# A two-layer hybrid backbone on one core: gathers between the turn of the activations and the down products, and the turn of a modulation group as a step of its own

## The reference

```python
for l in range(DEPTH):                       # DEPTH = 2, context and latent tokens alike
    sh1, sc1, g1, sh2, sc2, g2 = adaln_params(c, w_mod[l], b_mod[l])  # silu(c) @ w_mod: 1024 x 6144
    h = rmsnorm(x, ln1_g[l]) * (1 + sc1) + sh1
    conv, attention, mLSTM inputs and gates = split(h @ w_in[l])
    x = x + g1 * (concat(conv_o, na_o, ml_o) @ w_out[l])
    h2 = rmsnorm(x, ln2_g[l]) * (1 + sc2) + sh2
    # 16 experts in 4 groups: best group, 2 experts in it
    a = silu(h2 @ w_gate[e]) * (h2 @ w_up[e])
    x = x + g2 * sum_e gate[e] * (a @ w_down[e])
```

## Time and profile before

| | |
|---|---|
| median of three runs | 1233.97 us (1231.61 to 1316.1) |
| the profiled execution | 1231.81 us, of which the span is 1230.0 us |
| PE busy | 1145.1 us, 93% of the span |
| DVE, ACT, POOL busy | 409.4, 250.2, 56.5 us |
| mean granted clock of PE | 0.975 |
| moved | 315.15 MB, mean 256 GB/s; read from HBM 310.92 MB |

### The profile page before, as it was taken

The page is one execution under the profiler, slowest core; times in us unless marked ns, Lnnn a source line. Parts: engine busy times, 40 slices in busy tenths (PEclk is TensorE's granted clock), DMA queues, the critical chain, the costliest instruction groups (busy, mean ns, idle before and its releaser), DMA issues.

```text
span 1230.0 us, 15289 instructions
## 1 busy us (share of the span) xinstructions
PE 1145.1 (93%) x6240; PEld 623.2 (51%) x6240; DVE 409.4 (33%) x1150; ACT 250.2 (20%) x515; POOL 56.5 (5%) x82
## 2 busy tenths in 40 slices
PE   3999999898989999999989999998998999999996
PEld 3546555576544533554434564566654554355333
DVE  4402041355270333223252302224727032322234
ACT  2210121152132010110142011214413201011013
POOL 1230000000002000000020000000000000000001
PEclk8999999999999999999999999999998999999998
DMA  8967452277248989999971346234425698999991
GB/s 318 357 131 285 167 206 99 95 269 234 80 201 304 409 319 412 413 413 413 404 264 69 137 161 229 99 137 172 117 72 205 251 410 319 411 412 413 413 379 52
DMA packets 95512, 315.15 MB, mean 256 GB/s; under 512 B 5980, under 2 KB 6352, under 8 KB 86608
## 3 DMA queue, kind: packets, MB, share of 16 engines
q1 hardware_dynamic: 91856, 306.43, 65.1%
q0 software_dynamic: 3584, 7.71, 2.7%
HBM read 310.92 MB, written 4.99 MB: 257 GB/s over the span
## 4 chain that ended last, share of the span: by engine, by line
PE 85%; DVE 8%; ACT 3%; issue 2%; POOL 1%; DMA 1%; SPq 0%; DVEq 0%; POOLq 0%; ACTq 0%
PE ps L1341 18%; PE ps L944 16%; PE ps L1388 9%; PE ps L954 9%; PE ps L1112 6%; PE ps L1179 5%; PE ps L901 3%; PE ps L1207 2%; PE ps L891 2%; PE ps L1208 2%; PE ps L1231 1%; PE ps L1078 1%; PE ps L1143 1%; PE ps L934 1%; PE ps L1005 1%
## 5 line engine op out<-in xcount | busy, mean ns | idle before, releaser
L944 PE MATMUL ps<-ring,hT 128*128 128x512 f32 (+1 forms) x480 | 194.9, 565 | 0.0
L1341 PE MATMUL ps<-ring,arena 128*64 128x512 f32 x576 | 175.4, 595 | 0.0
L2014 DVE SCALAR_TENSOR_TENSOR xT<-ps,modT,xT 128x128 f32<-128x128 f32 x320 | 109.3, 410 | 193.9 <-PE ps L1208 106.0
L1341 PE MATMUL ps<-slot,arena 128*64 128x512 f32 x368 | 147.4, 596 | 0.0
L944 PEld LDWEIGHTS ps<-ring,hT 128*128 128x128 f32 x480 | 90.5, 190 | 98.0 <-issue 94.7
L954 PE MATMUL ps<-hT,ring 128*128 128x384 f32 x320 | 106.2, 489 | 0.0
L1388 PE MATMUL ps<-ring,arena 128*64 128x512 f32 x336 | 88.5, 613 | 8.1 <-ACT arena L1673 8.1
L1341 PEld LDWEIGHTS ps<-ring,arena 128*64 128x64 f32 x576 | 52.2, 137 | 78.9 <-issue 78.9
L1112 PE MATMUL ps<-mixT,ring 128*128 128x384 f32 x256 | 83.4, 487 | 1.7 <-ACT mixT L1601 1.7
L2238 DVE SCALAR_TENSOR_TENSOR y_low<-ps,route,y_high 128x512 fp32r<-128x512 f32 x32 | 23.9, 751 | 173.3 <-ACT y_high L1679 172.6
L954 PEld LDWEIGHTS ps<-hT,ring 128*128 128x128 f32 x320 | 59.8, 190 | 40.7 <-issue 0.8
(11 more groups left out here) (332 smaller groups left out, 1294.5 us busy)
## 6 DMA issues: line engine op xcount, KB each, us to landing
ring<-in_w_mod SPq DMA_DIRECT2D x24, 2048.0 KB, 11.7
ring<-in_w_down SPq DMA_DIRECT2D x44, 1024.0 KB, 13.7
ring<-in_w_up SPq DMA_DIRECT2D x40, 1024.0 KB, 11.3
ring<-in_w_gate SPq DMA_DIRECT2D x32, 1024.0 KB, 12.8
slot<-in_w_gate SPq DMA_DIRECT2D x30, 1024.0 KB, 13.1
ring<-in_w_in SPq DMA_DIRECT2D x14, 2048.0 KB, 12.3
slot<-in_w_up SPq DMA_DIRECT2D x22, 1024.0 KB, 10.3
slot<-in_w_down SPq DMA_DIRECT2D x22, 1024.0 KB, 11.3
```

What stands on the lines that cost most here:

```text
L944: mm = pe.matmul(p[:, 0:n], hT[:, k, t * P:(t + 1) * P], w[:, k, c0:c0 + n], start=(k == 0), stop=(k == KT - 1))
L1341: mm = pe.matmul(out[which][64 * s:64 * s + 64, :], xg[:, k, cols[s]], w[i][:, k % 4, :], start=(k == 0), stop=(k == KT - 1))
L2014: ins = dve.scalar_tensor_tensor(xT[:, m, cols], p[:, cols], modT[:, L, gate0 + m, j:j + 1], xT[:, m, cols], ALU.mult, ALU.add)
```

## The change

Two things are moved; nothing is added or removed in the arithmetic.

In the pairs, `aT` comes before the gathers on PE and on ACT. In the mixing half, the turn of a group is a step `mod_turn` of its own, one step behind the group's last block: behind the context scores for group 1, behind the turn of the last probabilities for group 2, behind `read(6)` for the next layer's group 0. And the four blocks of the next layer's group stand ahead of the reads 0, 2, 4 and 6 instead of 1, 3, 5 and 7.

```diff
     for dh in range(8):
         steps += [("decay", dh + 1)] if dh < 7 else []
-        steps += mods[:1] if dh % 2 else []
+        steps += mods[:1] if dh % 2 == 0 else []
         steps += [("read", dh)]
-        if dh % 2:
+        if dh % 2 == 0:
             del mods[:1]
     assert not mods
+    for i in reversed([i for i, step in enumerate(steps) if step[0] == "mod" and step[2] % 4 == 3]):
+        steps.insert(i + 2, ("mod_turn", *steps[i][1:]))
     return steps
...
                     if c % 4 == 3:
                         done(mm, name)
-                        bk.wait_drained(pe, name)
-                        turned = ("modT", which, c // 4)
-                        p = begin(turned)
-                        for i in range(4):
-                            mm = pe.transpose(p[:, i * P:(i + 1) * P], modrow[:, i * P:(i + 1) * P], ident)
-                        done(mm, turned)
                     else:
                         mm.then_inc(ly.mod_read, 1)
+
+                def mod_turn(which, c):
+
+                    bk.wait_drained(pe, ("mod", which, c // 4))
+                    turned = ("modT", which, c // 4)
+                    p = begin(turned)
+                    for i in range(4):
+                        mm = pe.transpose(p[:, i * P:(i + 1) * P], modrow[:, i * P:(i + 1) * P], ident)
+                    done(mm, turned)
...
                     done(mm, ("gs", j))
+                    bk.wait_drained(pe, ("U", j))
+                    p = begin(("aT", j))
+                    for f in range(4):
+                        mm = pe.transpose(p[:, f * P:(f + 1) * P], act_in[:, interleaved(f, 2)], ident)
+                    done(mm, ("aT", j))
                     if j in GATHER_AFTER:
...
                                         [2 * x, 2 * x + 1]), ("gB", part, x))
-                    bk.wait_drained(pe, ("U", j))
-                    p = begin(("aT", j))
-                    for f in range(4):
-                        mm = pe.transpose(p[:, f * P:(f + 1) * P], act_in[:, interleaved(f, 2)], ident)
-                    done(mm, ("aT", j))
                     bk.wait_drained(pe, ("aT", j))
                     out = [begin(("y", j, y)) for y in range(2)]
...
+                    p = full_of(("aT", j))
+                    drain(("aT", j), act.copy(aT, p[:, :]))
                     if j in GATHER_AFTER:
...
-                    p = full_of(("aT", j))
-                    drain(("aT", j), act.copy(aT, p[:, :]))
...
                     p = full_of(("mod", which, q))
                     drain(("mod", which, q), dve.tensor_copy(modrow[:], p[:, :]))
+
+                def mod_turn(which, c):
+
+                    q = c // 4
                     p = full_of(("modT", which, q))
```

More of the change, by code:

```diff
@@ L1096, in _ @@
                         mod(0, c)
+                    mod_turn(0, 3)
                     pe.wait_ge(const_loaded, 32)
-                steps = {"gates": gates, "by_token": by_token, "by_feature": by_feature, "mod": mod,
+                steps = {"gates": gates, "by_token": by_token, "by_feature": by_feature, "mod": mod, "mod_turn": mod_turn,
                          "gate_columns": gate_columns, "old_keys": old_keys, "turn": turn,
@@ L1978, in _ @@
                 norm(0)
-                steps = {"gates": gates, "mod": mod, "rope": rope, "by_feature": by_feature,
+                steps = {"gates": gates, "mod": mod, "mod_turn": mod_turn, "rope": rope, "by_feature": by_feature,
                          "context_scores": context_scores, "scores": scores, "context_turn": context_turn,
```

## The result

The changed kernel takes **1216.72 us** (median; 1215.09 to 1218.95), the kernel before in the same comparison 1233.8. The ratio is **0.9869**, 95% interval 0.9845 to 0.9892. The profiled execution took 1216.69 us, its span is 1214.8 us, its mean granted clock 0.978 (before: 0.975). One of the four runs of the kernel before, of 1316.1 us, is in a slower state of the chip and is not in the ratio.

The account below looks back on a forecast made before the run. PE was taken to bound the kernel, carrying 85% of the span; gains 3.1 + 3.8 + 3.2 + 6.0 = 16.1 us off 1231.8 gave 1215.7, plus 1 for the median: 1216.7; own range 1212 to 1219, 8 in 10 1210 to 1224.

Parts of the forecast that it names:

- Pairs: Gathers put between the turn and the down products in six pairs: 0.51 us gained a pair, 3.1 us in all.
- the 0.17 taken: PE's wait in us before the turn for VectorE's product, as seen in pair 5, replacing a 0.68 us wait.
- The reserve of the transfers: The tightest weight chunk lands 1.7 us before PE needs it; rival that transfers take back the gain: 1219.8, chance 0.12.
- A: Group 1's turn behind the context scores, once a layer: bias table 1.0 us earlier, clock stays high; 2 x 1.9 = 3.8 us.
- the rival: The clock stays low at A, which then gives 2.0 us; sum 14.3, time 1218.5; chance 0.17.
- The price of the clock at A: Each low stretch taken as worth 0.9 us; the skill's half gives 1.7, time 1.6 lower; PE-alone rival 1215.1, chance 0.06.
- B: Group 2's turn behind the last probabilities, once a layer: VectorE's normalising ends 1.6 us earlier; 2 x 1.6 = 3.2 us.
- C: Layer 0's decays: next layer's group products in even steps, its turn behind the read of step 6; 6.0 us gained.
- signs of being wrong: PE waiting for a transfer in pair 7, turns in pairs 0, 3, 4 waiting over 0.5 us, or newly low clock.

## Why the prediction came out right, point by point

The time forecast, 1216.7, is the one measured, and to hit it so closely is luck in part. The places and their mechanisms are as forecast, but as a sum it is right partly by errors that cancel. The places gave 18.2 us and not 16.1, and the clock took 4.4 back elsewhere. The profiled executions differ by 15.1 us, of which 1.1 are from their start and 1.0 from their end (there the clock is low over the last transposes before, and not after), which the change does not touch. The same kernel, run again, took 1219.51, just outside the forecast's own range.

- **Pairs**: forecast 3.1, measured 0.51 to 0.62 a place, 3.2 in all. The turn waits the 0.17 taken. The reserve of the transfers was not drawn on; they moved with PE.
- **A**: forecast 2 x 1.9, measured 2.14 and 2.33. Its two halves are as predicted where the clock holds: the first scores come 1.13 earlier (169.41 to 167.19, less 1.09), and 1.01 more by the second (173.33 to 170.10). The bank behind which the second scores stand came free 0.97 earlier, not 0.75, so the turn's later addition cost less than taken. That the clock stays high there holds in one execution and not in the next: in layer 0 it fell in five of ten traces, and the gain with it low, 0.82 to 1.07, is the rival's 1.0. So forecast and rival were both true, by the run, and the rival's chance of 0.17 was too small for layer 0.
- **The price of the clock at A**: the Trainium skill's "TensorE: Matmul & The Clock Gate", section "HAM oscillation — how this bites in real kernels", made of 3.4 us low 1.7. The two traces differ by 2.14 - 1.07 = 1.07, where the prediction took 0.9 from the row. The row was nearer. Over layer 1's decays, where PE was busy all the time, 6.8 us low cost 3.15. That is near the half of that page.
- **B**: forecast 2 x 1.6, measured 2.46 and 2.15. The normalising of layer 0 came 1.68 earlier (246.38 to 241.47, less 3.23), against the 1.6 taken. The rest there, 0.78, is a term that the sum lacks, the low clock before (244.7 to 248.1):

```profile
245.62 1.92 PE L891 MATMUL ps<-cst 128*128 128x512 f32 x2
247.33 0.85 PE L1022 MATMUL ps<-cst,arena 128*128 128x128 f32 x3
```

A product that nobody uses, which the kernel has there to keep PE busy, was still under way at half the clock when the normalising ended at 246.80, so the probabilities began 0.53 later; now they begin 0.05 behind it. The transposes themselves took 0.85 and take 0.55.
- **C**: forecast 6.0, measured 5.85, with 1.9 at the first read, VectorE's copy at once, L2006 4.0 earlier (296.09 to 286.39, less 5.69; forecast 4.14), and 4.61 from there.
- **The step that failed**: the sum has the clock as a gain at A and as no loss anywhere. A fall of the granted clock in stretches where it was 1.00 was one of the prediction's signs of being wrong, and it came: 3.15 us behind the first read of layer 1, 1.27 over the last scatters of layer 0. The first was there to be read: the same wait of 1.88 us that I filled in layer 0 stays in layer 1, next behind the low stretch that B takes away; in five of six traces the clock fell behind it.

The Trainium skill, same page, section "What's actually happening", says that the point at which the clock changes varies from run to run with the moment at which work starts. The two traces of the changed kernel agree: the clock fell at place A of layer 0 in one and not in the other.

## What to carry to other kernels

Take the wait that a change removes, then look at the next wait behind it: if the clock used to fall at the first, it can now fall at the second, and cost more than was gained (at place B of layer 1, 3.15 us lost against 2.15 gained). Taking that wait away as well, here by moving the sigmoid off the way to it into idle time, pays twice: 2.0 us of wait and 3.3 of clock. And before a step is moved off, ask what it covers: the turn of a group was worth its 0.6 us where it stood.

## What the hardware showed that I had not expected

- Within one kernel the time follows the mean granted clock: 0.978 goes with 1223.92 us and 0.970 with 1231.4, in twelve runs of the same program.
- Over a row of 48 products with 64 columns each the granted clock fell to 0.51 with PE busy for 6.80 of 6.80 us; over the same products among those of 512 columns it was 1.00, and fell for 3.4 us some 15 us behind them.
- Two products on the two halves of PE's columns run side by side, 0.9 us for both (3.65 for eight); one alone between other products takes 1.00.
